# A preparation loop reordered, and a router in one pipeline and one block of engines, in a two-block transformer kernel on one core

## The reference, cut to what matters

```
c_q, c_kv, k_rope, ... = split_columns(h @ w_in)
q = (rms_norm(c_q, q_a_norm) @ w_q_up).reshape(B, S, 8, 96)
kv = (rms_norm(c_kv, kv_a_norm) @ w_kv_up).reshape(B, S, 8, 128)
q, k = rms_norm(q, q_norm), rms_norm(concat(k_nope, k_rope), k_norm)   # rotary embedding behind it
r = rms_norm(o, o_norm) * silu(hg)                                     # the recurrence's output

t = rms_norm(x, norm_ffn)                    # 1024 x 1024
g_logits = t @ w_group + b_group             # 8 groups: the best one, with its softmax weight
e_logits = t @ w_expert + b_expert           # 64 experts: the best two of that group
for each token and each of its two experts:
    y += weight * (silu(t @ w_gate[e]) * (t @ w_up[e])) @ w_down[e]
```

## Time and profile before

| | us |
|---|---|
| median of 3 runs | 3726.07 |
| the profiled execution | 3719.99 |
| its span (first to last instruction) | 3718.0 |
| preparation (turns of 8 tiles) | 507 to 631 |
| from the last addition of the cross attention to the first expert matmul | 1356 to 1482 |
| loop over the experts | 1482 to 2001 |
| PE busy | 3186.8 (86% of the span) |
| mean granted TensorE clock | 0.919 of full speed |

### The profile page before, as it was taken

The page is one execution under the profiler, slowest core; times in us unless marked ns, Lnnn a source line. Parts: engine busy times, 40 slices in busy tenths (PEclk is TensorE's granted clock), DMA queues, the critical chain, the costliest instruction groups (busy, mean ns, idle before and its releaser), DMA issues. The chain is left out here.

```text
span 3718.0 us, 35575 instructions
## 1 busy us (share of the span) xinstructions
PE 3186.8 (86%) x14326; PEld 2322.1 (62%) x14326; DVE 1404.7 (38%) x2145; ACT 911.8 (25%) x1446; POOL 156.4 (4%) x220
## 2 busy tenths in 40 slices
PE   7995777998898874887874789899998989999997
PEld 6784743445676554322321667788777778888886
DVE  3125845784433323111112664551225233333334
ACT  3324334443323230000000222012132132122221
POOL 0000011000000000111110120000000000000000
PEclk9996878999899985999987799999999989999999
DMA  3110000002130015999995212211112111111112
GB/s 91 48 43 9 1 13 0 1 1 102 34 108 18 23 60 215 371 421 421 416 410 200 79 60 50 68 48 49 35 51 79 52 40 51 46 51 46 51 46 74
DMA packets 138914, 369.97 MB, mean 100 GB/s; under 512 B 45632, under 2 KB 59584, under 8 KB 112640
## 3 DMA queue, kind: packets, MB, share of 16 engines
q1 hardware_dynamic: 129552, 351.12, 26.1%
q0 software_dynamic: 9216, 16.80, 1.2%
HBM read 352.66 MB, written 32.79 MB: 104 GB/s over the span
## 5 line engine op out<-in xcount | busy, mean ns | idle before, releaser
L2334 PE MATMUL moe_ph<-moe_wgu,moe_rowsT 128*64 128x512 f32 x1024 | 264.0, 675 | 68.3 <-DMA moe_wgu<-in_moe_w_up_dram 39.4
L516 PE MATMUL mlp_ps<-mlp_high,mlp_w_cut 128*128 128x512 f32 x1024 | 317.0, 391 | 6.0 <-DVE mlp_w_cut L431 6.0
L516 PE MATMUL mlp_ps<-mlp_w_cut,mlp_hidden_high 128*128 128x512 f32 x1024 | 315.3, 389 | 0.0
L431 DVE TENSOR_TENSOR m_w_cut<-m_w_raw,m_w_cut 128x512 fp32r<-128x512 f32 (+1 forms) x92 | 94.3, 1029 | 454.5 <-ACT m_w_cut L427 454.2
L431 DVE TENSOR_TENSOR mlp_w_cut<-mlp_w_raw,mlp_w_cut 128x1024 fp32r<-128x1024 f32 x64 | 78.3, 1225 | 398.8 <-ACT mlp_w_cut L427 398.3
L2334 PEld LDWEIGHTS moe_ph<-moe_wgu,moe_rowsT 128*64 128x64 f32 x1024 | 84.3, 154 | 227.8 <-issue 201.2
L427 ACT ACTIVATE m_w_cut<-m_w_raw 128x512 fp32r<-128x512 f32 (+1 forms) x92 | 76.4, 835 | 605.3 <-PE m_gates_ps L516 196.4
L516 PEld LDWEIGHTS mlp_ps<-mlp_high,mlp_w_cut 128*128 128x128 f32 x1024 | 193.2, 189 | 46.5 <-DVE mlp_w_cut L431 6.4
L516 PEld LDWEIGHTS mlp_ps<-mlp_w_cut,mlp_hidden_high 128*128 128x128 f32 x1024 | 192.3, 188 | 39.9
L516 PE MATMUL mlp_ps<-mlp_low,mlp_w_cut 128*128 128x512 f32 x512 | 199.9, 390 | 0.0
L516 PE MATMUL mlp_ps<-mlp_w_cut,mlp_hidden_low 128*128 128x512 f32 x512 | 199.2, 389 | 0.0
(11 more groups left out here) (524 smaller groups left out, 5928.2 us busy)
## 6 DMA issues: line engine op xcount, KB each, us to landing
moe_wgu<-in_moe_w_gate_dram SPq DMA_DIRECT2D x64, 1024.0 KB, 19.1
...
mlp_w_raw<-in_w_ff_dram SPq DMA_DIRECT2D x64, 512.0 KB, 3.5
...
m_w_raw<-in_w_in_dram SPq DMA_DIRECT2D x20, 512.0 KB, 3.7
x_w_raw<-in_x_w_kv_dram SPq DMA_DIRECT2D x16, 512.0 KB, 3.6
```

The lines of the kernel that those rows point to most:

```text
L431: nc.vector.tensor_tensor(part(s, 1).bitcast(F32R), raw(s), part(s, 0), ALU.subtract).then_inc(low_ready, 1)
L516: ins = nc.tensor.matmul(ps[:, b, :r.shape[-1]], l, r, start=(k == 0 and sw is high and wh == 0), stop=(k == job.nk - 1 and sw is low))
L2334: ins = self.nc.tensor.matmul(self.ps_h[r, i].rearrange("p (i n) -> p i n", i=2), self.rowsT[:, i, k, r], self.wgu[:, w * self.parts + h, ...
```

## The change

**Preparation.** The same instructions in another order on two engines. On DVE `take_low(i + 1)` moves up to stand behind the sum of k, the sum of q moves behind the copies into `kT`, and `hg_sum(i + 1)` moves to the end of the turn. On ACT `hg_root(i + 1)` moves to the end of the turn.

**Router.** `router_logits` is new and replaces the gain's load, the router's loads, the norm and the logits. It is one block: SP starts all small loads, then the expert weights of two pairs. ACT takes square and root tile by tile, and starts the stores of `ffn_rows` itself, now from three buffers. DVE inverts, scales with the reordering of channels (L2114 of the changed kernel) and copies out times the gain (L2125), two tiles of scaling ahead. PE alternates between turning tile m (L2157) and the logits of tile m - 1 (L2139), which now have the 72 columns of the weights stationary and 128 tokens moving, so the logits come out turned; ACT copies four tiles of them out, PE turns them back (L2146) and DVE adds the bias (L2130). `route` is then one block with semaphores where blocks ended. PE's L2241 (before L2208) starts behind the 32 comparisons that it needs, beside DVE's overflow counts. The gather buffers are cleared in the loop's own block, one at a time, and the overflow block uses the loop's buffers, so both `clear_rows` blocks go.

```diff
@@ -1472,8 +1472,6 @@
...
-                    if i + 1 < NT:
-                        hg_root(i + 1)
@@ -1489,6 +1487,8 @@
...
+                    if i + 1 < NT:
+                        hg_root(i + 1)
@@ -1526,7 +1526,7 @@
...
                         if i + 1 < NT:
-                            hg_sum(i + 1)
+                            take_low(i + 1)
@@ -1539,17 +1539,17 @@
...
-                        if i + 1 < NT:
-                            take_low(i + 1)
-                        dve.wait_ge(q_squared, i + 1)
-                        nc.vector.tensor_reduce(rq[:, :, i], q_sq[i % 2], AX, ALU.add).then_inc(q_summed, 1)
                     if i:
...
+                    if i < NT:
+                        dve.wait_ge(q_squared, i + 1)
+                        nc.vector.tensor_reduce(rq[:, :, i], q_sq[i % 2], AX, ALU.add).then_inc(q_summed, 1)
                     if i + 1 < NT:
+                        hg_sum(i + 1)
                         hg_norm(i + 1)
...
+def router_logits(c, a, x, hT, gain, weights, xn, wr, bias, lg):
...
+    c.recycle(0)
...
+    BUF = 3
...
+        junk, normed = s("junk", [P, D]), s("normed", [P, BUF, D])
...
+        def take(act, h):
+            act.wait_ge(made, 4 * (h + 1))
+            nc.scalar.activation(lgT[:, h * CH:(h + 1) * CH], ps_l[:NE, h], ACT.Copy).then_inc(taken, 1)
...
+                with nc.allow_non_contiguous_dma("small parameters"):
+                    for t, src in loads:
+                        sp.dma_start(t, src).then_inc(loaded, 16)
                 for n in range(2):
                     load_expert_weights(sp, a, weights, n, 2, 2 * n)
...
+            @block.scalar
+            def _(act):
+                def root(m):
+                    nc.scalar.activation(junk[:], x[:, m], ACT.Square, accum_out=ssq[:, m:m + 1]).then_inc(summed, 1)
+                    act.wait_ge(summed, m + 1)
+                    nc.scalar.activation(rstd[:, m:m + 1], ssq[:, m:m + 1], ACT.Sqrt, bias=c.eps[:, 0:1],
+                                         scale=1.0 / D).then_inc(rooted, 1)
+                for m in range(3):
+                    root(m)
+                for m in range(NT):
+                    act.wait_ge(row_ready, m + 1)
+                    nc.scalar.dma_start(xn[m * P:(m + 1) * P, :], normed[:, m % BUF]).then_inc(kept[m % BUF], 16)
+                    if m + 3 < NT:
+                        root(m + 3)
+                    if m % 4 == 0 and m:
+                        take(act, 0)
+                take(act, 1)
...
+            @block.vector
+            def _(dve):
+                def scale(m):
+                    dve.wait_ge(rooted, m + 1)
+                    nc.vector.reciprocal(rstd[:, m:m + 1], rstd[:, m:m + 1]).then_inc(inverted, 1)
+                    if m >= BUF:
+                        dve.wait_ge(turned, m - BUF + 1)
+                        dve.wait_ge(kept[m % BUF], 16 * (m // BUF))
+                    dve.wait_ge(inverted, m + 1)
+                    nc.vector.tensor_scalar(normed[:, m % BUF].rearrange("t (k p) -> t p k", p=P),
+                                            x[:, m].rearrange("t (p k) -> t p k", p=P), rstd[:, m:m + 1], None,
+                                            ALU.mult).then_inc(row_ready, 1)
+                scale(0)
+                scale(1)
+                dve.wait_ge(loaded, 16 * len(loads))
+                for m in range(NT):
+                    if m + 2 < NT:
+                        scale(m + 2)
+                    dve.wait_ge(turned, m + 1)
+                    nc.vector.tensor_tensor(hT[:, :, m * P:(m + 1) * P], sums(m),
+                                            gain[:].unsqueeze(2).to_broadcast([P, KD, P]),
+                                            ALU.mult).then_inc(evacuated, 1)
+                for h in range(2):
+                    dve.wait_ge(back, h + 1)
+                    nc.vector.tensor_tensor(lg[:, 4 * h:4 * h + 4], ps_b[:, h, :4 * NE].rearrange(
+                        "p (m n) -> p m n", n=NE), bias[:].to_broadcast([P, 4, NE]), ALU.add)
...
+                def logits(m):
+                    pe.wait_ge(evacuated, m + 1)
+                    at = slice(m * P, (m + 1) * P)
...
+                        ins = nc.tensor.matmul(ps_l[:NE, m // 4, (m % 4) * P:(m % 4 + 1) * P], wr[:, k], hT[:, k, at],
...
+                    ins.then_inc(made, 1)
+                def turn_back(h):
+                    pe.wait_ge(taken, h + 1)
+                    for m in range(4):
+                        ins = nc.tensor.transpose(ps_b[:, h, m * NE:(m + 1) * NE],
+                                                  lgT[:, h * CH + m * P:h * CH + (m + 1) * P], c.ident[:NE, :NE])
+                    ins.then_inc(back, 1)
+                pe.wait_ge(loaded, 16 * len(loads))
+                for m in range(NT + 1):
+                    if m < NT:
+                        pe.wait_ge(row_ready, m + 1)
+                        if m >= 2:
+                            pe.wait_ge(evacuated, m - 1)
+                        for k in range(KD):
+                            ins = nc.tensor.transpose(ps[:, 2 * (m % 2) + k // 4, (k % 4) * P:(k % 4 + 1) * P],
+                                                      normed[:, m % BUF, k * P:(k + 1) * P], c.ident[:])
+                        ins.then_inc(turned, 1)
+                    if m:
+                        logits(m - 1)
+                    if m == 6:
+                        turn_back(0)
+                turn_back(1)
...
+def route(c, a, lg, w1, w2, slot_tok, slot_row, ov_expert, ov_count, weights):
...
+            @block.scalar
+            def _(act):
+                for k, t in enumerate((ex, m2)):
+                    act.wait_ge(exps, k + 1)
+                    nc.scalar.activation(t[:], t[:], ACT.Exp).then_inc(exps_done, 1)
...
+            @block.tensor
+            def _(pe):
+                pe.wait_ge(made, 7)
+                pe.wait_ge(picked, 1)
...
+                    ins = nc.tensor.matmul(ps[:, 1, :E], ones[:], both[:, i], start=(i == 0), stop=(i == NT - 1))
+                ins.then_inc(ranked, 1)
+                pe.wait_ge(placed, 1)
...
+                ins.then_inc(filled, 1)
...
+                v = nc.vector
                 do(nc.vector.tensor_reduce(gm[:], lg[:, :, 0:G], AX, ALU.max))
-                do(nc.vector.tensor_tensor(ex[:], lg[:, :, 0:G], gm[:].unsqueeze(2).to_broadcast([P, NT, G]),
-                                           ALU.subtract))
-        with nc.Block() as block:
...
+                nc.vector.tensor_tensor(ex[:], lg[:, :, 0:G], gm[:].unsqueeze(2).to_broadcast([P, NT, G]),
+                                        ALU.subtract).then_inc(exps, 1)
+                dve.wait_ge(made, 7)
...
-                do(nc.vector.tensor_tensor(m2[:], m2[:], m1[:], ALU.subtract))
+                nc.vector.tensor_tensor(m2[:], m2[:], m1[:], ALU.subtract).then_inc(exps, 1)
...
-                do(nc.vector.tensor_tensor(both[:], flat[0], flat[1], ALU.add))
-        with nc.Block() as block:
-            @block.scalar
...
-        with nc.Block() as block:
-            @block.vector
...
+                nc.vector.tensor_tensor(both[:], flat[0], flat[1], ALU.add).then_inc(picked, 1)
+                dve.wait_ge(exps_done, 2)
...
+                dve.wait_ge(ranked, 1)
...
+                        ins = v.tensor_scalar(atblk[:, k, m], idsb[:], blk[:, k, m:m + 1], val[:, k, m:m + 1],
+                                              ALU.is_equal, ALU.mult)
+                ins.then_inc(placed, 1)
...
-        with nc.Block() as block:
-            @block.tensor
...
-        with nc.Block() as block:
-            @block.vector
-            def _(dve):
...
+                dve.wait_ge(filled, 1)
...
+        if like:
+            self.rows, self.rowsT, self.itok, self.irow = like.rows, like.rowsT, like.itok, like.irow
+            self.gated, self.hid, self.hidT, self.res = like.gated, like.hid, like.hidT, like.res
...
-            load(c, [(gain[:], a["norm_ffn"][0].rearrange("(p k) -> p k", p=P))])
-            c.recycle(0)
-            loaded = c.sem("router_loaded")
...
-            with nc.Block() as block:
...
-            norm_transpose(c, "ffn", x, hT, gain, NT, keep=xn)
-            route(c, a, hT, w1[:], w2[:], slot_tok[:], slot_row[:], ov_expert[:], ov_count[:], weights,
...
+            lg = sbuf(tmp, nc, "rt_logits", [P, NT, NE])
+            router_logits(c, a, x, hT, gain, weights, xn, wr, bias, lg)
+            route(c, a, lg, w1[:], w2[:], slot_tok[:], slot_row[:], ov_expert[:], ov_count[:], weights)
...
-            clear_rows(c, st.rows)
+            cleared = c.sem("moe_rows_cleared")
...
+                        pool.wait_ge(cleared, n + 1)
...
+                    for b in range(BUFS):
+                        nc.vector.memset(st.rows[:, b], 0.0).then_inc(cleared, 1)
...
-        c.recycle(0)
-        with ExitStack() as run:
+            c.recycle(0)
...
```

(3 more changed lines are left out.)

118 lines of the change are left out of this document (49 added, 69 removed).

## The result

| | before | changed |
|---|---|---|
| median of 4 runs, us | 3725.23 (3713.9 to 3727.59) | 3663.34 (3657.88 to 3666.64) |
| profiled execution / its span, us | 3719.99 / 3718.0 | 3664.36 / 3662.6 |
| mean granted clock | 0.919 | 0.929 |

The ratio is 0.9834 (95% interval 0.9819 to 0.9849): 61.9 us faster by the medians, 55.4 by the spans. (The 6 us between the two figures come mostly from the profiled execution of the kernel before, which was 5 us quicker than its median.)

The account below looks back on a forecast made before the run. It took DVE's order to bound the preparation, a serial chain the router, and weights the experts' loop. Savings of 11.7 + 15 + 9.8 + 1.7 = 38.2 us gave 3681.8, plus 6.1 to the median: 3688 us, range 3670 to 3705.

Parts of the forecast that it names:

- Preparation: Eight turns before attention: reordering saves 11.7 us; bounds 0, and up to 3.3 us more per low-clock turn.
- Two sums leave the stretch ahead of the first `kT` copy: Preparation: moving hg's sum (about 0.6 us) and q's (0.86) saves 1.5 us in each of turns 1 to 6.
- Router pipeline: Router's norm and logits, tile by tile: logits end at 1408.7 instead of 1423.6, 15 us earlier.
- Scaling: Router: DVE's scaling of a tile with reordered channels, taken as 2.1 us; the contiguous kind takes 0.75.
- PE bounds with 4.7 us a tile: Router pipeline: 1.6 us of transposes plus 3.1 of logits at a mixed clock, against 3.6 for DVE.
- second rival: High clock: 10 us more from the preparation and 9.5 from the router, 3668 us; 12%.
- Joints: Waits and block changes within `route`, up to the experts: 9.8 us saved.
- tail: Behind the experts: a clearing block and part of a block change go, 1.7 us saved, bounds 0.9 and 2.5.
- the stream moving whole: Experts' weights: a shorter router moves the whole stream forward, each microsecond saved ahead being saved at the end too.
- Rival 3: Router: stores beside the weights hold the buffers, hidden at 9.6 us each; otherwise the pipeline's 15 us are lost, 3703; 8%.
- rivals 1, 4 and 5: Low clock throughout, 3698 (15%); weights' total deciding the loop's end, 3713 (3%); no overlap in the router pipeline, 3736 (2%).
- Rival 5: Router pipeline without overlap, 11.5 us a tile: logits end near 1457, 33 us late, kernel 3736 us; 2%.

Follow-up runs that it names:

- early_qsum: The changed kernel with q's sum put back ahead of the kT copies in the preparation; 3689.46 us.
- fill: The changed kernel with eight spare transposes of the identity on TensorE in each turn of the preparation; 3655.33 us.
- stores_first: The changed kernel with SyncE's waits for the stores of the normed rows ahead of the loads of the first two pairs' weights; 3650.83 us.
- pairs: The changed kernel with TensorE's last product of the router released pair by pair, not after all 32 placed operands; 3658.83 us.
- tokens: The kernel of stores_first with the logits' tokens stationary and the 72 columns of the router's weights moving; 3653.05 us.
- new_prep: The kernel before with the changed order of the preparation alone; 3695.84 us.
- all_warm: The kernel of all with 36 spare transposes of the identity on TensorE at the start of the router; 3649.31 us.
- all: The changed kernel with the changes of fill, stores_first, tokens and pairs, and the router's small loads waited for apart; 3647.84 us.

## Why the prediction was wrong

The direction and both places were right; two terms of the sum were mis-sized, and their order was the other way round (the prediction had the router's pipeline ahead of the preparation).

- **Preparation, 11.7 forecast, 23.9 measured.** The costing at equal clock held: 1.63 us for an inner turn (1.5), 1.7 for the first (2.0), 0.9 for the last (0.9), 12.4 in all. What failed is "Bounds: 0, and with the clock kept high in more turns up to 3.3 us": I carried the clock as an upper bound and as half of a rival of 12%, and took nothing of it into the sum, though the earlier trace rows showed both levels side by side and the earlier trace rows the wait of the low turn. `early_qsum` and `fill` show that it belongs to the step itself. It was 11.5 us, nearly as much as the order's own part.
- **The same term, right for a wrong reason.** "Two sums leave the stretch ahead of the first `kT` copy" was read off a low turn, and there it holds: from the start of k's sum to the first copy VectorE takes 4.27 us in the turn of the earlier trace rows (576.30 to 580.57) and 2.80 in a low turn of the changed kernel (578.94 to 581.74), 1.47 less. At the high clock hg's sum was hidden, and it is `take_low`'s 0.8 that leaves. That the two are nearly as long is luck.
- **Router pipeline, 15 forecast, 20.1 measured.** Scaling: 1.34 us, within the bounds of 0.75 and 2.1 but not at the end that I took, so the reordering costs 0.6 us over the contiguous kind and not 1.35. "PE bounds with 4.7 us a tile": wrong, tiles follow one another in 2.6 us at the high clock (`stores_first`), and the clock was 0.89 (the second rival's assumption). Instead of it the stores set 3.7 a tile, over 5 for the first two. From TensorE's start to the end of the logits it was 31.6 us where the prediction has 40.6. Two smaller terms took 1.9 us each of those 9.0 back: TensorE started 9.9 us behind the last addition and not 8.0, since the last load needed 6.4 us instead of 3.8 beside the weights, and what stands behind the logits took 5.6 us and not 3.7.
- **"At 9.6 us, three tiles per 9.6 + 2.3 is 4.0 us a tile, under 4.7, so it hides"**: the stores took 11.5, and with TensorE at 2.6 a tile nothing hid them. By `stores_first` they cost up to 9 us of the change's possible gain, and the loads beside the weights 3. The errors in TensorE's pace and in the stores pointed opposite ways, which left only 5 us.
- **Joints 9.8, tail 1.7, the stream moving whole**: 9.9, 1.5, and a loop of the same 512.8 us. Right, and `pairs` confirms what is on VectorE's path there.
- **Second rival, 3668 at 12%**: its mechanism (less waiting, higher clock) is what happened, at 24 us instead of 22 in the preparation and with 5 of its 9.5 in the router. It deserved a share of the forecast. Rival 3 was right in kind too, and masked by the faster tiles; rivals 1, 4 and 5 did not show. (Rival 5 sets the logits' end, 1457, against 1423.6, which is the end of two operations behind them; with its own 3.7 us it would be 37 us late.)

The Trainium skill (TensorE: Matmul & The Clock Gate, section "What's actually happening") says that sustained matmul activity releases the throttle to 2.4 GHz, and I set it aside on the row of 26 us at 0.53. Here `fill`, `tokens` and both kernels with the logits apart agree with it; the 26 us, the 27.6 of `new_prep`, and the 11 us at 0.53 in `all_warm` do not. By the rule alone I would have forecast 3668, and have been nearer.

The Trainium skill (DMA: Bandwidth & Descriptors, section "Issuing engines are not separate DMA queues") says that DMAs issued by different engines share the same 16 engines. The stores' 11.5 us beside the weights and 2.7 without agree.

**What stays open** is what brings the clock down and back in each single case. A wait lowers it often and not each time (turns of the changed kernel with much the same waits ran at 0.70 and 1.00), it stayed down for 11 us of work without a wait in `all_warm`, and neither the order of the work nor the stream of weights explains by itself the 26 us at the lower level in the kernel before. The side that moves is not excluded: all four traces with such long stretches in the router have 72 columns moving, and no run changes that side alone at the low level. If it is the cause, a part of the router's gain belongs to the turned logits, and `all` lost time by turning them back.
